# A Strassen pooling layer on one core: when row blocks, row operands and pooling steps are handled

## The reference, cut to what matters

```
uz = rmsnorm(x, g_norm) @ w_in                      # (2080, 1024) @ (1024, 4096)
u, z = uz[..., :2048], uz[..., 2048:]
# four channel groups of 512, trailing windows 2, 4, 8, 16 over the positions
mix = window_mean(u) - u
mix = einsum('btgi,gio->btgo', mix, w_map) * scale  # one 512 x 512 map for each group
x + (mix * silu(z)) @ w_out
```

## Time and profile before

| | |
|---|---|
| time, median of 3 runs | 2913.86 us |
| runs | 2909.94, 2913.86 and 5648.6 us |
| profiled execution | 2909.62 us |
| its span | 2907.9 us |
| PE, DVE, ACT, POOL busy | 96%, 66%, 49%, 15% of the span |
| mean granted TensorE clock | 0.99 |

### The profile page before, as it was taken

The page is one execution under the profiler, slowest core; times in us unless marked ns, Lnnn a source line. Parts: engine busy times, 40 slices in busy tenths (PEclk is TensorE's granted clock), DMA queues, the critical chain, the costliest instruction groups (busy, mean ns, idle before and its releaser), DMA issues. The chain is left out here.

```text
span 2907.9 us, 45393 instructions
## 1 busy us (share of the span) xinstructions
PE 2798.3 (96%) x16738; PEld 2329.8 (80%) x16738; DVE 1924.0 (66%) x2858; ACT 1420.8 (49%) x2313; POOL 449.2 (15%) x370
## 2 busy tenths in 40 slices
PE   8998989899999999999999999999999999999998
PEld 7776768787877888888888888879999999865787
DVE  3466777878863232477667666588888888754654
ACT  5554434433332221455646454367777777733322
POOL 1223434355510000000000000100000000012321
PEclk9999999999999999999999999999999999999999
DMA  8743323445346766487988878873444444599543
GB/s 280 234 158 98 124 89 139 143 149 167 118 162 224 235 209 211 180 293 267 302 276 267 271 257 257 260 166 80 111 101 108 108 101 102 196 382 415 204 177 109
DMA packets 329991, 562.01 MB, mean 193 GB/s; under 512 B 25545, under 2 KB 237113, under 8 KB 307385
## 3 DMA queue, kind: packets, MB, share of 16 engines
q1 hardware_dynamic: 327745, 559.24, 59.6%
q0 software_dynamic: 2048, 0.14, 0.0%
HBM read 404.90 MB, written 155.12 MB: 193 GB/s over the span
## 5 line engine op out<-in xcount | busy, mean ns | idle before, releaser
L1278 PE MATMUL pool_acc<-at_pool_x_hi,at_pool_w_hi 128*128 128x512 f32 x896 | 357.3, 399 | 46.5 <-DVE at_pool_ext L1041 27.0
L1279 PE MATMUL pool_acc<-at_pool_x_lo,at_pool_w_hi 128*128 128x512 f32 x896 | 352.6, 394 | 0.0
L1280 PE MATMUL pool_acc<-at_pool_x_hi,at_pool_w_lo 128*128 128x512 f32 x896 | 352.4, 393 | 0.0
L2715 ACT ACTIVATE attn_scores<-attn_scores,attn_lowest 128x1024 f32<-128x1024 f32 (+15 forms) x256 | 306.7, 1202 | 0.0
L2776 DVE CUSTOM_DVE_ANT_0 attn_scores<-attn_s,region_early 128x1024 f32<-128x1024 f32 (+7 forms) x256 | 216.5, 856 | 67.9 <-PE attn_s L2654 37.8
L1278 PEld LDWEIGHTS pool_acc<-at_pool_x_hi,at_pool_w_hi 128*128 128x128 f32 x896 | 170.9, 191 | 89.7 <-issue 53.6
L289 PE MATMUL outa_acc<-outa_w_hi,outa_g_hi 128*128 128x512 f32 x512 | 201.2, 393 | 6.7 <-DVE outa_w_lo L1644 4.0
L290 PE MATMUL outa_acc<-outa_w_lo,outa_g_hi 128*128 128x512 f32 x512 | 199.9, 390 | 0.0
L1280 PEld LDWEIGHTS pool_acc<-at_pool_x_hi,at_pool_w_lo 128*128 128x128 f32 x896 | 170.4, 190 | 36.6
L291 PE MATMUL outa_acc<-outa_w_hi,outa_g_lo 128*128 128x512 f32 x512 | 199.7, 390 | 0.0
L1279 PEld LDWEIGHTS pool_acc<-at_pool_x_lo,at_pool_w_hi 128*128 128x128 f32 x896 | 170.9, 191 | 34.4
(11 more groups left out here) (391 smaller groups left out, 6801.2 us busy)
## 6 DMA issues: line engine op xcount, KB each, us to landing
region_early<-w_fold SPq DMA_DIRECT2D x110, 1024.0 KB, 6.5
region_early<-in_cache_v SPq DMA_DIRECT2D x44, 512.0 KB, 7.9
hold_kq<-in_cache_k SPq DMA_DIRECT2D x40, 512.0 KB, 7.6
w_fold<-region_early SPq DMA_DIRECT2D x22, 896.0 KB, 5.9
at_pool_raw<-w_mix SPq DMA_DIRECT2D x16, 1024.0 KB, 5.5
at_pool_raw<-in_w_in_a SPq DMA_DIRECT2D x16, 1024.0 KB, 5.4
gatedT<-at_pool_z SPq DMA_DIRECT2D x32, 512.0 KB, 2.6
region_early<-gatedT SPq DMA_DIRECT2D x16, 1024.0 KB, 5.6
```

The costliest lines, as they stand in the source:

```text
L1278: pe.matmul(bank[i], a, c, start=first, stop=False, skip_group_check=begun)
L1279: pe.matmul(bank[i], a, d, start=False, stop=False, skip_group_check=begun)
L1280: x = pe.matmul(bank[i], b, c, start=False, stop=end, skip_group_check=begun)
L2715: act.activation(part, part, ACT.Exp, scale=-1.0, bias=low[s][:, x:x + 1], accum_out=sums[s][:, i:i + 1]).then_inc(expd, 1)
```

## The change

- `pool_steps` uses a list of slots that leaves slot 4 out: slots 0 to 3 and 5 to 8, or 0 to 3, 5 and 6 for the last unit that is pooled.
- SP loads a unit's row block (`norm.load`) ahead of the stores of that unit, where it stood behind them.
- Each step on a row block comes later. In the block's own unit, ACT's square is at product 5 (before: at 3) and DVE's average at product 6 (before: at 4). In the next unit, ACT's root is at product 0 (before: at product 5 of the own unit), DVE's scaling at product 1 (before: at product 6 of the own unit), PE's transposes follow product 2 (before: product 0), and ACT's move into the stage is at product 4 (before: at 2).
- `row_operand_at(q)` gives the places of `x_high` and `x_low`. In unit 0 these are products 0, 1, 3 and 4 as before. Operands 7 to 13 come at products 1, 3 and 5 of unit 15 and 0, 2, 3 and 5 of unit 16 (before: 1, 2, 5, 6 and 0, 1, 2). On ACT `x_high` now stands behind `take_first` and `take_11` of the same product, where it stood ahead of them.
- `sample_map(x)` takes the map product of the sample rows out of `rows_step`: for groups 0 to 2 of the preface order it comes at k = 7 and its transpose at k = 0 of the next group (before: 6 and 7); for the last group nothing moves. SP's load of the map two groups on moves from k = 6 to k = 7.

No instruction is added or taken away on any engine, and no tile changes its place or size.

```diff
         def pool_steps(n, i):
-            slots = 7 if n == LAST - 1 else 9
+            slots = (0, 1, 2, 3, 5, 6) if n == LAST - 1 else (0, 1, 2, 3, 5, 6, 7, 8)
             count = 2 * pool_length(n)
-            return [k for k in range(count) if k * slots // count == i]
+            return [k for k in range(count) if slots[k * len(slots) // count] == i]
...
+        def map_step(x):
+            for g in range(NG):
+                at = g * KC + (KC - 1 if g + 1 < NG else KC - 2)
+                if x - at in (0, 1):
+                    return g, x - at
+            return None, None
...
+        def row_operand_at(q):
+            if q < 7:
+                return {0: 3, 1: 4, 3: 5, 4: 6}.get(q)
+            return {106: 7, 108: 8, 110: 9, 112: 10, 114: 11, 115: 12, 117: 13}.get(q - 7 * (VN - 16))
...
         def on_sp(sp):
...
-                if k == 6 and g + 2 < NG:
+                if k == 7 and g + 2 < NG:
                     sp.wait_ge(m_made, g + 1)
                     sp.wait_ge(map_lo_made, (g + 1) * GC)
                     self.load_map(sp, g + 2)
...
             for n in range(NU):
...
+                b = norm_block_at(n)
+                if b is not None:
+                    norm.load(sp, b)
                 if kind == "u" and n:
                     store(n - 1, 0)
                     store(n - 1, 1)
...
-                b = norm_block_at(n)
-                if b is not None:
-                    norm.load(sp, b)
                 p, r = pair_at(n - 3)
                 if r == 0:
                     store_x(p)
...
         def on_act(act):
...
                     w_high(q + 2)
-                    if n == 0 and i in (0, 1, 3, 4):
-                        x_high({0: 3, 1: 4, 3: 5, 4: 6}[i])
-                    for j in range(7):
-                        if q == 7 * (VN - 1) + j + 1 + (2 if j >= 2 else 0):
-                            x_high(7 + j)
...
                     if i == 3:
                         take_11(n)
+                    y = row_operand_at(q)
+                    if y is not None:
+                        x_high(y)
...
+                    b = norm_block_at(n - 1)
+                    if b is not None and i in (0, 4):
+                        norm_step(b, {0: 1, 4: 4}[i])
                     b = norm_block_at(n)
-                    if b is not None and i in (3, 5):
-                        norm_step(b, {3: 0, 5: 1}[i])
-                    b = norm_block_at(n - 1)
-                    if b is not None and i == 2:
-                        norm_step(b, 4)
+                    if b is not None and i == 5:
+                        norm_step(b, 0)
...
         def on_dve(dve):
...
+                    b = norm_block_at(n - 1)
+                    if b is not None and i == 1:
+                        norm_step(b, 1)
                     b = norm_block_at(n)
-                    if b is not None and i in (4, 6):
-                        norm_step(b, {4: 0, 6: 1}[i])
+                    if b is not None and i == 6:
+                        norm_step(b, 0)
...
         def on_pe(pe):
...
                     b = norm_block_at(n - 1)
-                    if b is not None and i == 0:
+                    if b is not None and i == 2:
                         norm.turn(pe, b)
```

22 lines of the change are left out of this document (13 added, 9 removed).

## The result

| | before | changed |
|---|---|---|
| median of the runs | 2910.58 us | 2876.36 us |
| lowest, highest | 2909.94, 2913.86 | 2871.43, 2877.24 |
| ratio to before, 95% interval | 1 | 0.9878 [0.9861, 0.9895] |
| profiled execution, its span | 2909.62, 2907.9 us | 2877.24, 2875.5 us |

I had forecast 2869 us, 2853 to 2887. The time fell into the range, 7 us above the forecast. Two of my own tests for being wrong were met all the same, and what stood behind them is the better half of this study.

What follows compares the result with a forecast made beforehand. It took PE to set the time, so gains lay only in its waits in preface and main stage, at most some 62 us. Terms summed to 42.0 us off the 2907.9 us span, giving 2869 us, range 2853 to 2887.

Steps and rivals of the forecast that it cites:

- tests for being wrong: Wrong if `w_lo` or scaled-row waits exceed 5 us in sum, or block 11/15's square ends over 3 us behind product 6's start.
- block loaded ahead: Units 2 and 8: loading the row block ahead of the stores removes both long waits; gain 10.3 us.
- square behind the stage's store: Units 4 and 10: the store lands earlier, leaving only a 0.7 us wait in unit 10; gain 20.5 us.
- no slot 4: Units 9, 21, 23, 25, 27: product 6 no longer waits for additions behind a pooling step; gain 5.7 us.
- moved scalings: Units 3, 5, 9, 11: DVE's scalings moved there from `u` units cost 3 us, bounds 0 and 7.2.
- unit 0: Copy of bank 21 stops waiting for operand 4, but product 6 waits some 3.6 us; gain 0.5 us, bounds 0 and 5.8.
- row operands, unit 16: Unit 16: operands placed nearer to their use, yet products 4 to 6 late; gain 3.4 us, bounds 0 and 10.4.
- map product: Preface: the later map product saves PE waiting in two of three places; gain 2.1 us, bounds 0 and 5.4.
- small things: Main stage: remaining idle time and slower first matmuls behind long waits; gain 2.5 us, bounds 0 and 4.
- DVE becomes the bound: Rival, chance 0.06: slots with two pooling steps make DVE late in 16 `z` units, costing 77 us, time 2946 us.
- by DVE's durations alone: Alternative view of the scalings moved into units 3, 5, 9, 11: their 3 us cost would be nothing.
- What I said would show it: Main stage signs: about 650 us, `ext` waits under 4, `z` under 1.5, units 2, 4, 8, 10 none above 1.

Runs made afterwards that it cites:

- a_psum: Changed kernel with the unused output of the square for row blocks 9 to 16 in the transposing banks instead of the stage; 2865.94 us, ratio to before 0.9858.
- a_half: Changed kernel with the old nine pooling slots for the first half, the list without slot 4 only for the second; 2870.00 us, ratio to before 0.9868.
- p_slots: Kernel before with only the pooling slots changed, leaving out slot 4; 2905.42 us, ratio to before 0.9986.
- a_halfload: Changed kernel loading only half of the bytes of row operands 9 to 13; 2876.28 us, ratio to before 0.9887.
- a_gates: Changed kernel with only the gates of unit 15 moved, from products 2 and 3 to 5 and 6 of unit 16; 2873.26 us, ratio to before 0.9874.
- p_blocks: Kernel before with only the row block part: load ahead of the stores and the block's steps later; 2879.18 us, ratio to before 0.9898.

## Why the prediction was right, and where not

The span fell by 32.4 us where my sum had 42.0. The total held since the terms that I overrated (units 10 to 12, unit 16) were partly made up by ones that I underrated, and since the range was 34 us wide; that much was luck. Term by term, gain in us, forecast against the units:

| term | forecast | measured |
|---|---|---|
| block loaded ahead (units 2, 3, 8, 9) | 10.3 | 13.4 |
| square behind the stage's store (4, 5, 10 to 12) | 20.5 | 7.5; with the row blocks alone 15.2 |
| no slot 4 | 5.7 | 6.2 in units 21 to 27; 6.1 lost in units 4, 5, 10 and 12, contained in the row above |
| moved scalings | -3 | none as a unit's time |
| unit 0 | 0.5 | 1.4 |
| row operands, unit 16 | 3.4 | 0.6 |
| map product | 2.1 | 3.45; alone 2.4 at the start (which varies by 1 to 2 us) |
| small things | 2.5 | -0.1 in all units not named (1.15 - 1.26) |

**The step that failed** is the one on the stage's store: "The first product that needs them is now product 1 of unit 5 [...]: no wait." As far as it goes it was nearly right. The landing took 7.8 us from the issue, and I had 7.5; unit 5's product 1 waited 0.7, unit 11's 1.41 where I had 0.7. It stopped too early. I followed the weight operands behind the square, but not the block itself: the average, the root, the scaling and the transposes now had one or two products between them where the square had only just run. PE waited for the scaled row, 1.21 us in unit 5 and 2.63 in unit 11, and behind the longer one came the low clock. a_psum, which only frees the square from the store, gives 2.3 and 6.0 us back in exactly these two units. That is the first half of the missing gain.

**The second half** is the slots. "The step comes back at products 5 and 6, where DVE has two products in hand" is true of the second half of the rows, and its units 21, 23, 25 and 27 are clean. In the first half a unit has up to 14 steps; two doublings in slot 6 took 3.45 us beside POOL, ahead of the next unit's weights. I had priced exactly such a slot in the rival "DVE becomes the bound", 3.8 to 5.7 us against 2.72 for a product, and then let it go with "unit 9 alone is near full". a_half shows that units 4, 5, 10 and 12 lose 6.1 us by it, and p_slots that even alone it costs 3.9 in units 10 and 12. The rival was right in mechanism (the steps stand in the `z` unit's part of the list, the wait shows mostly at the head of the next unit), wrong in extent (four units instead of sixteen, 6 us instead of 77), so the chance of 0.06 for a slower kernel was no misjudgment, but its small version belonged into the sum.

**Unit 16** was mis-sized, not misread. I had products 4, 5 and 6 late by 0.8, 1.8 and 3.9 us; they were late by 1.5, 2.3 and 4.6, and the low clock cost 2.5 more at product 6 itself instead of the 0.5 that I took. I had added up the links of the transfer chain; a_halfload and a_gates show that DVE's list was the longer one.

**The scalings** that I charged with 3 us, by the port rule of the Trainium skill, cost next to nothing that PE sees: units 3 and 9 take 21.38 us in p_blocks, and in a_psum all four `z` units with a scaling do, which is the clean value. The rule (SBUF — State Buffer, "Who interferes with whom") has DVE and GpSimd take turns on a shared pair of ports, and the durations agree with it. Scalings take 0.75 us with no addition of POOL beside them and 1.57 to 1.80 in six of the eight cases of the main stage. A scaling reads one tensor in SBUF and one value for each partition, so the reason that I gave, two inputs in SBUF, isn't the one that this section of the Trainium skill has for it: there `tensor_scalar` comes into it by its two-port modes. But where the block is in time, 1 us more for DVE is hidden. Only in unit 5, where the block is late for its transposes already, can it show: the scaling takes 1.57 us right ahead of the wait of 1.21, at most 0.8 us of it. Going "by DVE's durations alone", the other side of that comparison, would have given the better sum for this term.

**What I said would show it.** The main stage in about 650 us: 661.2. No wait above 1 us in units 2, 4, 8: right; unit 10: wrong (1.52). `z` waits below 1.5: right, the name has left the list. `ext` under 4: missed, 4.5. Unit 16 waiting at products 4 to 6 for row operands and not for bank 21: right. And the two tests for being wrong: waits for `w_lo` and the scaled row came to 6.9 + 4.5 us, above 5; and the square of block 11 ended at 259.2, 5 us behind the start of product 6 (256.94 - 2.72 = 254.2), above 3. Both pointed at the right places. I had drawn no consequence for the sum from either.

## What to carry to other kernels

When a stall is cured by moving a step later, follow what the step *produces* to its last consumer, not only what stands behind it in its queue: here the operands behind the square were nearly in time and the transposes of its own block were not. Where a step waits for a transfer only because of where its unused output goes, changing that place is worth trying beside the moves: it gave 8.3 us in the units on top of them, and 8.8 us by itself on the kernel before. And before moving work about inside a stretch, compare each engine's busy time there with the bound's: at 43.6 of 50.7 us, order could give 7 us at the most, and the orders tried here gave 2 to 3.
